# Strassen's block products moved from between the chunks into the down product

## The reference, cut to what matters

```python
h2 = _rmsnorm(x, norm2_w) * (1.0 + scale2) + shift2
ffn = jnp.dot(jax.nn.silu(jnp.dot(h2, w_ffn_gate)) * jnp.dot(h2, w_ffn_up), w_ffn_down)
x = x + gate2 * ffn
return _rmsnorm(x, final_norm_w)
```

## Time and profile before

| | |
|---|---|
| median of 3 runs | 1418.01 us (1417.1 to 1418.36) |
| profiled execution | 1416.94 us, its span 1415.1 us |
| PE busy | 1401.8 us (99%) |
| VectorE, ScalarE, GpSimd busy | 956.5, 731.7, 160.1 us |
| granted TensorE clock | 0.999 of 2.4 GHz |
| DMA | 288.24 MB, 204 GB/s on average |

### The profile page before, as it was taken

One profiled execution on the slowest core, in us unless ns is written; L12 is line 12 of the kernel. 1 busy time (PEld: TensorE's weight loads), 2 busy tenths in 40 slices (PEclk: granted clock), 3 DMA queues, 4 the chain that ended last, 5 costly groups with the idle time before them and its releaser, 6 DMA issues.

```text
span 1415.1 us, 19090 instructions
## 1 busy us (share of the span) xinstructions
PE 1401.8 (99%) x7327; PEld 1147.2 (81%) x7327; DVE 956.5 (68%) x1307; ACT 731.7 (52%) x1050; POOL 160.1 (11%) x242
## 2 busy tenths in 40 slices
PE   9999999999999999999999999999999999999997
PEld 7888888688888888888878888888877788888886
DVE  6666567886676667665787757755568566786654
ACT  6444455564443445543665545445655634655542
POOL 1600010000000000000172100000542110011000
PEclk9999999999999999999999999999999999999999
DMA  9585755256876778868544688764845355588551
GB/s 318 199 253 198 262 203 207 68 171 207 251 242 215 231 228 265 252 210 264 187 150 148 203 210 256 255 211 140 238 160 197 121 178 179 171 242 211 178 209 59
DMA packets 234857, 288.24 MB, mean 204 GB/s; under 512 B 37076, under 2 KB 156672, under 8 KB 234768
## 3 DMA queue, kind: packets, MB, share of 16 engines
q1 hardware_dynamic: 232160, 281.48, 61.6%
q0 software_dynamic: 2208, 5.24, 1.8%
q10 hardware_dynamic: 400, 0.31, 0.1%
HBM read 282.80 MB, written 4.20 MB: 203 GB/s over the span
## 4 chain that ended last, share of the span: by engine, by line
PE 95%; DVE 2%; issue 1%; ACT 1%; POOL 0%; POOLq 0%; ACTq 0%; DVEq 0%
PE ps L706 29%; PE ps L709 28%; PE ps L707 28%; PE pst L974 1%; PE pst L1155 1%; DVE wlo L532 1%; PE pst L1468 1%; PE ps L813 0%; PE ps L812 0%; PE ps L811 0%; PE ps L1415 0%; ACT whi L521 0%; PE ps L679 0%; PE pst L1782 0%; PE pst L2355 0%
## 5 line engine op out<-in xcount | busy, mean ns | idle before, releaser
L532 DVE TENSOR_TENSOR wlo<-raw,whi 128x1024 fp32r<-128x1024 f32 (+2 forms) x468 | 558.2, 1224 | 257.7 <-ACT whi L521 255.9
L521 ACT ACTIVATE whi<-raw 128x1024 fp32r<-128x1024 f32 (+2 forms) x468 | 467.8, 1040 | 244.2 <-PE ps L709 97.4
L706 PE MATMUL ps<-whi,xh 128*128 128x512 f32 (+4 forms) x1406 | 551.5, 392 | 1.6 <-ACT xh L1013 0.6
L707 PE MATMUL ps<-wlo,xh 128*128 128x512 f32 (+4 forms) x1406 | 541.1, 385 | 0.0
L709 PE MATMUL ps<-whi,xl 128*128 128x512 f32 (+4 forms) x1406 | 532.7, 385 | 0.0
L706 PEld LDWEIGHTS ps<-whi,xh 128*128 128x128 f32 x1406 | 263.9, 188 | 60.6 <-issue 4.7
L709 PEld LDWEIGHTS ps<-whi,xl 128*128 128x128 f32 x1406 | 263.9, 188 | 53.6
L707 PEld LDWEIGHTS ps<-wlo,xh 128*128 128x128 f32 x1406 | 264.2, 188 | 49.8
L706 PE MATMUL ps<-whi,gh 128*128 128x512 f32 x440 | 172.0, 391 | 0.0
L707 PE MATMUL ps<-wlo,gh 128*128 128x512 f32 x440 | 171.2, 389 | 0.0
L709 PE MATMUL ps<-whi,gl 128*128 128x512 f32 x440 | 153.4, 389 | 0.0
(11 more groups left out here) (306 smaller groups left out, 956.0 us busy)
## 6 DMA issues: line engine op xcount, KB each, us to landing
raw<-in_ffn_w_in_dram SPq DMA_DIRECT2D x174, 512.0 KB, 5.3
raw<-in_ffn_w_out_dram SPq DMA_DIRECT2D x40, 1024.0 KB, 5.5
raw<-in_w_in_dram SPq DMA_DIRECT2D x26, 1024.0 KB, 4.8
adat<-in_w_ada_dram SPq DMA_DIRECT2D x96, 256.0 KB, 2.8
raw<-in_hyb_w_in_dram SPq DMA_DIRECT2D x10, 1024.0 KB, 5.1
raw<-in_gla_w_in_dram SPq DMA_DIRECT2D x10, 1024.0 KB, 5.2
raw<-in_w_ffn_down_dram SPq DMA_DIRECT2D x10, 1024.0 KB, 5.0
raw<-in_w_ffn_gate_dram SPq DMA_DIRECT2D x18, 512.0 KB, 3.9
```

What stands on the lines that cost most here:

```text
L521: e.activation(split_of(whi, j), raw_of(j), ACT.Copy).then_inc(*whi_made.up(j))
L532: e.tensor_tensor(split_of(wlo, j), raw_of(j), split_of(whi, j).bitcast(F32), ALU.subtract).then_inc(*wlo_made.up(j))
L706: e.matmul(ps[:, 0:n], a, whi_of(j, k), start=first and k == 0, stop=False)
L707: last = e.matmul(ps[:, 0:n], a, wlo_of(j, k), start=False, stop=False)
```

## The change

In stage 7 the products leave the places between the chunks. p1 comes behind chunk 7, ahead of chunk 10; p5, p6, p3 and p2, p7, and p4 stand in the down product ahead of its sub units i = 2, 4, 6, 10 and 12. The down product of stage 7 goes by output columns over the first 16 blocks: all with n = 0, then all with n = 1; the last 6 blocks come in the order of before. The pair is turned ahead of i = 14 and first used at i = 16. PSUM banks are given out anew. The sums of x are made step by step during chunks 3 and 4 and split in two halves during chunk 5. The splits, the additions onto `rowx` and `workx` and `dve_t2` follow the new order.

Outside of stage 7: a column's sends, reads and fold of the modulation come one unit earlier each (behind units 10, 11 and 12 of its ten, not 11, 12 and 13); the gate rows are written by 8 DMAs of 128 elements at 8 units in a row, not by one of 1024; row g2 is loaded 6 units later, row g5 at the ninth unit of the down product.

```diff
+        BESIDE = {2: ("p5",), 4: ("p6",), 6: ("p3", "p2"), 10: ("p7",), 12: ("p4",)}
+        mixed_units = [(k, min(4, k1 - k), n) for k0, k1 in ((0, 16), (16, 22)) for n in range(2) for k in range(k0, k1, 4)]
...
-                return (0, 1, "p1", 2, "p2", 3, "p5", 4, "p6", 5, "p3", 6, "p7", 7, "p4", 10)
+                return (*range(8), "p1", 10)
...
         for c in range(12):
+            i = min(10 * c, c * (len(ada_units) - 13) // 11)
             for k in range(8):
-                ada_tiles[ada_units[10 * c + k]] = c, k
-            ada_sent[ada_units[10 * c + 11]] = c
-            ada_read[ada_units[10 * c + 12]] = c
-            ada_summed[ada_units[10 * c + 13]] = c
+                ada_tiles[ada_units[i + k]] = c, k
+            ada_sent[ada_units[i + 10]] = c
+            ada_read[ada_units[i + 11]] = c
+            ada_summed[ada_units[i + 12]] = c
...
             pool_product(e, st, "p1", False)
+            e.wait_ge(*xlo_made.at(st, "sums", 1))
+            pool_product(e, st, "p3", False)
             split("p1")
             pool_product(e, st, "p5", True)
-            e.wait_ge(*xlo_made.at(st, "sums"))
-            pool_product(e, st, "p3", False)
             split("p6")
             pool_product(e, st, "p4", True)
             split("p3")
...
-                "p1": ("a", 4, True, (silu_made, st, PAIR, 1)), "p2": ("b", None, False, None),
-                "p5": ("c", 5, True, (gated, st, PAIR, 1)), "p3": ("d", 3, False, (gated, st, PAIR, 0)),
+                "p1": ("a", 0, True, (silu_made, st, PAIR, 1)), "p2": ("b", None, False, None),
+                "p5": ("c", 1, True, (gated, st, PAIR, 1)), "p3": ("d", 5, False, (gated, st, PAIR, 0)),
...
                 if q == 0:
+                    if mixed:
+                        take(tok, n, acc.n + 2 + 2 * tok + n)
                     for done in freed[tok, n]:
                         e.wait_ge(*done)
...
             def at(i):
+                if st in STRASSEN:
+                    for name in BESIDE.get(i, ()):
+                        pe_product(e, st, name, acc.n)
+                    if i == 14:
+                        pe_hid_two(e, st, PAIR)
...
+        SX_AT = [(3, 0), (3, 1), (3, 2), (3, 3), (4, 0)]
+        SX_HI, SX_LO = [(5, 0), (5, 2)], [(5, 1), (5, 3)]
...
                 if i == 2:
                     act_ghi(e, st, 10)
+                if mixed and i in (5, 11):
+                    act_part(e, st, "p6" if i == 5 else "p7")
+                if mixed and i in (7, 13):
+                    act_silu_pair(e, st, i // 13)
+                if mixed and i == 15:
+                    act_ghi(e, st, PAIR)
...
+                if mixed and i in (5, 11):
+                    dve_combine(e, st, "p6" if i == 5 else "p7")
+                if mixed and i in (7, 13):
+                    dve_gate_pair(e, st, i // 13)
+                if mixed and i == 15:
+                    dve_glo(e, st, PAIR)
...
-                if u in (U0[5] + 10, U0[6] + 8):
-                    i, which = (0, 2) if u < U0[6] else (1, 5)
-                    e.wait_ge(*mod_made.at(2 * which + 1))
-                    e.dma_start(gate_rows[i].rearrange("(b p) -> p b", p=P), modc[:, which * 8:which * 8 + 8],
-                                allow_slow_non_contiguous=True).then_inc(*s_gates.up(which))
-                if u == U0[6] + 10:
+                if u in gate_piece:
+                    which, b = gate_piece[u]
+                    if b == 0:
+                        e.wait_ge(*mod_made.at(2 * which + 1))
+                    e.dma_start(gate_rows[which // 5][b * P:(b + 1) * P].rearrange("(p o) -> p o", o=1),
+                                modc[:, which * 8 + b:which * 8 + b + 1], allow_slow_non_contiguous=True
+                                ).then_inc(*s_gates.up(which))
+                if u == U0[6] + 16:
                     load_row(e, "g2", gate_rows[0], D, [s_gates.at(2), f_scaled.at(5, 1, 1)])
-                if u == (down_unit[7] if 7 in STRASSEN else U0[7] + 4):
+                if u == (down_units[7][8] if 7 in STRASSEN else U0[7] + 4):
                     load_row(e, "g5", gate_rows[1], D, [s_gates.at(5), gr_made.at(1, 1), *rows_free(7)])
```

More of the change, by code:

```diff
@@ L360, in program @@
         JD = {st: first_sub[u] for st, u in down_unit.items()}
+        DSUB = {JD[st]: [j for u in us for j in range(first_sub[u], last_sub[u] + 1)] for st, us in down_units.items()}
         JC = {key: first_sub[u] for key, u in chunk_unit.items()}
@@ L580, in sum_of, with dve_sx @@
             return workx[:, i * 512:(i + 1) * 512]
-        def dve_sx(e, st):
-            def whole(z):
-                return z[:, :].bitcast(F32).rearrange("p (k n) -> p k n", k=8)[:, :, 0:P]
+        def dve_sx(e, st, step):
             a11, a12, a21, a22 = (sum_of(name) for name in ("p6", "p3", "p7", "p5"))
[L587 to L597, removed]
@@ L599, in act_sx, with whole @@
-        def act_sx(e, st):
-            e.wait_ge(*summed.at(st, "x", "p3"))
[L601 to L605, removed]
+            if step == 0:
+                def whole(z):
+                    return z[:, :].bitcast(F32).rearrange("p (k n) -> p k n", k=8)[:, :, 0:P]
+                e.wait_ge(*squares.at(("h", st, 1), 1))
+                e.wait_ge(*xlo_made.at(st, 1, 3 if st == 7 else 1))
+                e.tensor_tensor(junk[:, :].rearrange("p (k n) -> p k n", k=8), whole(xh), whole(xl), ALU.add
+                                ).then_inc(*summed.up(st, "x", 0))
@@ new lines, in dve_sx @@
+            if step == 1:
+                e.tensor_tensor(a22, a21, a22, ALU.subtract).then_inc(*summed.up(st, "x", "p5"))
+            if step == 2:
+                e.wait_ge(*summed.at(st, "x", "p5"))
+                e.tensor_tensor(a21, a11, a21, ALU.subtract).then_inc(*summed.up(st, "x", "p7"))
+            if step == 3:
+                e.wait_ge(*summed.at(st, "x", "p7"))
+                e.tensor_tensor(a11, a22, a11, ALU.subtract).then_inc(*summed.up(st, "x", "p6"))
+            if step == 4:
+                e.wait_ge(*summed.at(st, "x", "p6"))
+                e.tensor_tensor(a12, a12, a11, ALU.add).then_inc(*summed.up(st, "x", "p3"))
@@ new lines, in act_sx, with dve_sx_lo @@
+        def act_sx(e, st, half):
+            o = slice(half * 1024, (half + 1) * 1024)
+            e.wait_ge(*summed.at(st, "x", "p3"))
+            e.activation(sxh[:, o], workx[:, o], ACT.Copy).then_inc(*xhi_made.up(st, "sums", half))
+        def dve_sx_lo(e, st, half):
+            o = slice(half * 1024, (half + 1) * 1024)
+            e.wait_ge(*xhi_made.at(st, "sums", half))
+            e.tensor_tensor(sxl[:, o], workx[:, o], sxh[:, o].bitcast(F32), ALU.subtract
+                            ).then_inc(*xlo_made.up(st, "sums", half))
@@ L788, in pe_product @@
             if name == "p1":
-                acc.next((st, "b"), (silu_made, st, PAIR, 0), tile=base + 2)
+                acc.next((st, "b"), (silu_made, st, PAIR, 0), tile=base + 3)
                 b_freed[st] = acc.freed
@@ L849, in pe_chunk, with down_sub, mixed_order @@
                     pe_part(e, bank[tok], j0 + i, xh, xl, 2 * i, 8, tok)
+        def down_sub(j0, i):
+            return DSUB[j0][i] if j0 in DSUB else j0 + i
+        def mixed_order():
+            return [(q, n) for k, m, n in mixed_units for q in range(k, k + m, 2)]
         def down_order(nk):
@@ L859, in pe_down, with take @@
             bank, freed = {}, {}
-            for tok in range(2):
-                for n in range(2):
-                    bank[tok, n] = acc.next((key, tok, n), *readers(tok, n))
-                    freed[tok, n] = acc.freed
-            order = down_order(nk)
+            def take(tok, n, tile=None):
+                bank[tok, n] = acc.next((key, tok, n), *readers(tok, n), tile=tile)
+                freed[tok, n] = acc.freed
+            mixed = j0 in DSUB
+            if not mixed:
+                for tok in range(2):
+                    for n in range(2):
+                        take(tok, n)
+            order = mixed_order() if mixed else down_order(nk)
             def one(i, tok):
@@ L1126, in dve_gate_pair, with before @@
                                    ).then_inc(*gated.up(st, PAIR, tok))
+        def before(st, c):
+            return 6 if c == 10 and st in STRASSEN else c - 2
         def turn_of(c):
@@ L1231, in act_ffn @@
             else:
-                act_open(e, st, before, lambda tok: act_silu(e, st, 0, tok))
+                act_open(e, st, opening, lambda tok: act_silu(e, st, 0, tok))
+            mixed = st in STRASSEN
             for c in sequence(st)[1:]:
@@ L1252, in act_ffn @@
             for i in range(22):
-                act_begin(e, JD[st] + i)
+                for name in BESIDE.get(i, ()) if mixed else ():
+                    for half in range(2):
+                        act_begin(e, JP[st, name] + half)
+                act_begin(e, down_sub(JD[st], i))
                 if i == 2:
                     act_ghi(e, st, 10)
```

(3 more changed lines are left out.)

88 lines of the change are left out of this document (44 added, 44 removed).

## The result

The changed kernel takes 1432.49 us (median of 4 runs, 1431.04 to 1434.8), the kernel before in the same session 1417.55 (4 runs, 1416.97 to 1418.36). The ratio is 1.0108, 95% interval 1.0093 to 1.0123: it is slower by 14.9 us. The profiled execution took 1434.8 us, its span is 1433.0, 17.9 more than before.

What follows compares the result with a forecast made beforehand. The prediction took PE's own matmul pace as the bound. Stage 7 and gate rows at 0 and stage 3's opening at 1.0 us put the span at 1417.9 and the median at 1419.0 us, range 1417.0 to 1422.5.

Steps and rivals of the forecast that it cites:

- PE's pace is the bound; stage 7 costs 0: Stage 7: PE's 780 matmuls at 0.227 us stay, the other engines work beside it; 0 us.
- The five new waits: Stage 7: new waits around p3, p4, i=8, the pair's turn and i=16, each with 3.2 to 4 us spare; 0.
- The gate rows: Eight issues of 0.43 us, each with about 0.9 us of the old 6.95 us ScalarE holdup, stay hidden; 0.
- the splits run four sub units (about 11 us) ahead of PE, which covers this.: Mid-stage: the splits' lead over PE covers SyncE's new waits around a column's sends and reads.
- Term A: Stage 3's opening, VectorE: the earlier fold delays xh of the second token tile; PE stalls about 0.25 us.
- Term B: Stage 3's opening, SyncE: waiting for sends delays unit 2's load and xh; 0.5 us, plus 0.25 on Term A.
- The estimate of 2.15 us: Skill's figure for a 64 KB send, set aside for the trace's 4.1 to 4.8; by it Term B would vanish.
- The sum of A and B: Stage 3's opening: 0.25 + 0.5 + 0.25 = 1.0 us, the whole forecast loss.
- Rival 2: Stage 3's opening costs more: unit 2's load stuck behind SyncE's wait for sends; 1421 to 1423 us, chance 0.09.
- Rival 3: Stage 7 gets a new wait, likeliest from p7's added block landing late; 1421 to 1425 us, chance 0.06.

Runs made afterwards that it cites:

- e4: Changed kernel with one DMA per gate row and the ada offsets as before, leaving stage 7's rewrite and the ada columns' spread; 1416.93 us, ratio 0.9999.
- e1: Changed kernel with each gate row sent by one DMA of 1024 elements again, early ada offsets kept; 1418.95 us, ratio 1.0015.
- n3: Changed kernel with stage 5's eight gate DMAs three units apart instead of one each unit; 1441.08 us.
- o1: Changed kernel with stage 5's eight gate DMAs moved from the chunks into its down product; 1431.97 us.
- m0: Kernel before with both gate rows in stage 6, one DMA each, g2 loaded later, and one 64 KB probe DMA in stage 5; 1420.2 us.
- m2: As m0, but with eight probe DMAs in stage 5, each 128 elements of 4 B, 512 B apart; 1419.31 us.
- m3: As m0, but with eight probe DMAs in stage 5, each 128 runs of 512 B (64 KB); 1417.68 us.

## Why the prediction was wrong, point by point

- **PE's pace is the bound; stage 7 costs 0.** Right. First matmul of the down product to 0.03 us, no wait behind the opening, e4 at 0.9999. The five new waits are all covered, and PE's 780 matmuls keep their pace.
- **The gate rows, "each with an eighth of that holdup", 0.** The step that failed, with 12.5 to 16 us of the loss. It scaled a DMA's landing by its elements, though the only row for it could not say whether the price went by DMA, by element or by address. The right bound from that row was a full holdup for each: 8 times 7 us. Its second half, "where all eight added up without recovery it would be 7 us once more, hidden again", kept that bound out: it multiplied eight by an eighth. And it called "hidden" what was 6.95 us of a lead of unknown length, not a wait of no consequence.
- **"the splits run four sub units (about 11 us) ahead of PE, which covers this."** Too large. What has to be covered is the silu that stands behind the splits in ScalarE's order, and in a chunk the ring gives back at most 0.6 us a unit.
- **Term A, 0.25.** Right in place and near in size: fold before the gain, PE waits 0.20 at 504.02. From 490 to 516 us the four traces with the early offsets lose 0.46 to 0.49 us, the others nothing. What it left out is the second effect, the 1.4 us passed on through buffer and load to the turn at 525.09: 1.8 us here, 0.8 to 1.1 in e1, n3 and o1. Up to 0.8 us of such a loss at this turn stands in traces with the old offsets too (m0), so how much the change has of it stays open.
- **Term B, 0.5 + 0.25.** Wrong, it gave 0: the sends start at 477.75, 2 us sooner than forecast, and take 2.57 us, the load of unit 2 leaves at 484.03, xh is not late. The row that misled is the earlier trace rows: with no load ahead of them the sends land in 2.0 to 2.2 us, not in 4.1 to 4.8. The estimate of 2.15 us, by which term B would vanish and which the prediction set aside, is what this place shows. (The Trainium skill, DMA: Bandwidth & Descriptors, Anatomy of one DMA, gives its figure for transfers issued by GpSimd; these are SyncE's.)
- **The sum of A and B,** forecast 1.0, measured 2.0 in the medians (e1 less e4), of which the traces give 0.7 to stage 3 and 1.1 to stage 5. B was nothing, and the second effect and stage 5's part were not in the forecast, so that the sum has at least the order of size is luck.
- **Rivals.** Rival 2 had the place in stage 3 and the wrong mechanism (its size, 2.8 us and more, wasn't reached there either). Rival 3 had a new wait, in the wrong stage. None named the gate DMAs, which had been costed at nothing.

## What to carry to other kernels

Price a DMA that is cut in pieces at its full landing for each piece until a row shows that the landing falls with size; writing single 4-byte elements densely into memory is a case where it hardly does (9.8 us in the median for 128, 11.0 for 1024). If a piece of work is hidden, find out how long the cover is and how fast it grows back (here 0.5 us a unit) before it is hidden eight times. Where an engine's program puts the work that feeds the next stage behind work that waits for a load, the loads' lead can end at that instruction, before the matmul that uses the load, as it did in the changed kernel's stage 5.

## What the runs showed of the hardware

Landing of a DMA of 4-byte elements from 128 partitions depends on how near they land: in the median 3.4 us at 512 B apart, 4.6 at 64 B, 9.9 to 11.0 when contiguous; 64 KB in runs of 512 B takes 4.1. While such a DMA is under way, 512 KB loads issued behind it land in 8.5 to 13.2 us instead of 5.5. A send of 64 KB lands in 2.3 to 2.6 us in the median of the kernels that issue it ahead of a load of weights, in 4.5 to 4.7 in those that issue it behind one. Behind the wait of 5.58 us TensorE ran at the lower of its levels for 4.0 us of matmuls (0.43 us between starts for 0.227), and behind that of 5.72 again; the two waits of 11.3 us cost 4.7 more, some 40% on top of their own length. The Trainium skill, DMA: Bandwidth & Descriptors, Rules for kernel authors, says to gather many small transfers into one. For the gate rows the runs agree, with 13.1 us between eight and one; but eight of 128 elements 512 B apart in the same places lost nothing in stage 5 (m2), nor did eight of 64 KB (m3).
